# A hybrid decoder block on one core: how the attention values are multiplied, where the probabilities are scaled, and where both stand in TensorE's order

## What is computed

```python
scores = jnp.einsum('bnqgrd,bnkgd->bgrnqk', qb, kk)          # 128 queries x 256 keys a block
scores = jnp.where(valid, scores, -jnp.inf)
m = jnp.maximum(jnp.max(scores, axis=-1, keepdims=True), sink)
pexp = jnp.exp(scores - m)
probs = pexp / (jnp.sum(pexp, axis=-1, keepdims=True) + jnp.exp(sink - m))
out = jnp.einsum('bgrnqk,bnkgd->bnqgrd', probs, vv)
```

## Time and profile before

| | us |
|---|---|
| median of 3 executions | 2165.63 |
| lowest, highest | 2164.36, 2166.37 |
| the profiled execution, its own time | 2168.98 |
| span of the profiled execution | 2167.4 |
| granted TensorE clock, mean over the span | 0.984 |

### The profile page before, as it was taken

How to read it: one execution, slowest core, us unless ns; L and a number is a source line. 1 busy time by engine, 2 the same in 40 slices (tenths; PEclk the granted TensorE clock), 3 DMA queues, 4 the chain that set the end, 5 groups by cost and what they waited for, 6 DMA issues and landing times. The chain is left out here.

```text
span 2167.4 us, 29054 instructions
## 1 busy us (share of the span) xinstructions
PE 2090.6 (96%) x10218; PEld 1739.7 (80%) x10218; DVE 1307.5 (60%) x1824; ACT 844.0 (39%) x1589; POOL 598.4 (28%) x600
## 2 busy tenths in 40 slices
PE   7999999979999999999979999999999999999997
PEld 6888889967878778778758888887888888878885
DVE  6854552237767767777743344558887777752523
ACT  5332221024454444454443222434444443443432
POOL 1000011146576666565610000004222222100000
PEclk9999999989999999999989999999999999999998
DMA  6122241223443433443355434321222222355343
GB/s 225 62 90 97 87 166 69 84 85 129 119 125 117 124 114 124 124 131 97 95 175 179 141 134 145 122 94 72 88 87 71 75 87 87 138 161 195 112 151 88
DMA packets 131264, 252.73 MB, mean 117 GB/s; under 512 B 25264, under 2 KB 70448, under 8 KB 131152
## 3 DMA queue, kind: packets, MB, share of 16 engines
q1 hardware_dynamic: 85584, 174.98, 24.9%
q0 software_dynamic: 15360, 55.32, 7.5%
q10 hardware_dynamic: 30208, 20.98, 3.0%
HBM read 189.63 MB, written 61.60 MB: 116 GB/s over the span
## 5 line engine op out<-in xcount | busy, mean ns | idle before, releaser
L155 PE MATMUL ps_zg<-u_hi,g_hi 128*128 128x512 f32 x448 | 186.0, 415 | 0.0
L157 PE MATMUL ps_zg<-u_hi,g_lo 128*128 128x512 f32 x448 | 177.1, 395 | 0.0
L156 PE MATMUL ps_zg<-u_lo,g_hi 128*128 128x512 f32 x448 | 176.2, 393 | 0.0
L2057 DVE TENSOR_TENSOR lt_d_lo<-lt_w_raw,lt_d_hi 128x640 fp32r<-128x640 f32 (+1 forms) x64 | 57.1, 892 | 147.2 <-ACT lt_d_hi L1782 142.5
L973 POOL TENSOR_TENSOR mx_seg<-mx_seg,mx_cbm 128x1024 f32<-128x1024 f32 x32 | 76.0, 2376 | 161.3 <-DVE mx_cbm L1130 161.3
L155 PE MATMUL ps_zg<-z_w,u_hi 128*128 128x512 f32 x256 | 108.6, 424 | 7.1 <-DVE mx_silu L1155 6.9
L155 PE MATMUL lt_ps<-lt_h_hi,lt_w_hi 128*128 128x512 f32 x256 | 100.7, 393 | 14.8 <-DVE lt_h_lo L2095 13.6
L157 PE MATMUL ps_zg<-z_w,u_lo 128*128 128x512 f32 x256 | 102.3, 400 | 0.0
L156 PE MATMUL ps_zg<-z_w,u_hi 128*128 128x512 f32 x256 | 101.8, 398 | 0.0
L1782 ACT ACTIVATE lt_d_hi<-lt_w_raw 128x640 fp32r<-128x640 f32 (+1 forms) x64 | 50.6, 791 | 130.5 <-PE lt_ps L157 119.6
L1656 POOL TENSOR_TENSOR lt_t_f<-lt_w_raw 128x512 f32<-128x512 f32 x21 | 29.1, 1385 | 261.7 <-DVE lt_t_lo L1985 260.2
(11 more groups left out here) (390 smaller groups left out, 6229.8 us busy)
## 6 DMA issues: line engine op xcount, KB each, us to landing
lt_w_raw<-in_w_up SPq DMA_DIRECT2D x44, 512.0 KB, 4.5
mx_a_row<-acs_s SPq DMA_DIRECT2D x32, 512.0 KB, 3.9
g_raw<-in_w_xbc SPq DMA_DIRECT2D x24, 512.0 KB, 3.2
lt_sig<-gate_s SPq DMA_DIRECT2D x24, 512.0 KB, 3.6
lt_w_raw<-in_w_down SPq DMA_DIRECT2D x32, 384.0 KB, 3.2
ff_s<-lt_fo SPq DMA_DIRECT2D x21, 512.0 KB, 5.0
tok_s<-fr_work POOLq DMA_DIRECT2D x20, 512.0 KB, 3.8
lt_w_raw<-in_w_down SPq DMA_DIRECT2D x32, 320.0 KB, 2.9
```

The source lines that it names most:

```text
L155: pe.matmul(dst, s_hi, m_hi, start=first, stop=False)
L156: pe.matmul(dst, s_hi, m_lo, start=False, stop=False)
L157: return pe.matmul(dst, s_lo, m_hi, start=False, stop=last)
L2057: dve.tensor_tensor(d_lo[:, m % 2, 0:n], w_raw[:, m % 2, 0:n], d_hi[:, m % 2, 0:n].bitcast(F32), ALU.subtract).then_inc(dw_lo_done, 1)
```

## The change

- `values` takes the value block as the weights (64 columns) and the turned probabilities of two heads as the moving operand (256 columns). The output goes to `ps_f` with the head's channels on the partitions: two heads in partitions 0 to 63, two in 64 to 127. It needs no transpose: the transposes of `o_tok`, `o_tok` itself and `attention_out` are gone, and `outputs` copies `o_t` from `ps_f` behind `pv_done`.
- The probabilities are scaled by 1/denominator before they are turned, by four copies with a scale on ScalarE, behind the gate's copy and store (and at c = 7 behind the high parts of the z weights). VectorE makes the reciprocal behind the state update, ahead of the sum of y.
- The transposes of the probabilities stand behind all 24 z products (k = 0 to 7) instead of behind 9 of them.
- `values` of n-1 stands behind gate products 0 to 3 instead of ahead of them, and waits for `ps_f`: for the state update of n-1, or at the end of a group for the copy of the outputs of n-2. The transposes of q and k no longer wait for `o_ready`.

The diff, cut to its core:

```diff
@@ scalar: outputs @@
-                act.wait_ge(o_turned, n + 1)
+                act.wait_ge(pv_done, n + 1)
@@ scalar: group @@
                     act.activation(sink_e[:], mx[:, 1], ACT.Exp).then_inc(sink_done, 1)
...
                     if c == NT - 1 and not last:
                         for k in range(4, KT):
                             split_z(g + 1, k)
+                    act.wait_ge(rden_ready, n + 1)
+                    for r in range(REP):
+                        ins = act.activation(sc[:, r, 0:keys], sc[:, r, 0:keys], ACT.Copy, scale=rden[:, r:r + 1])
+                    ins.then_inc(p_scaled, 1)
                     act.wait_ge(p_turned, n + 1)
@@ vector @@
-            def attention_out(n, opening):
...
-                    if not opening:
-                        attention_out(n - 1, first and c == 1)
...
                         dve.tensor_tensor(state[:], kept[:], ps_f[:], ALU.add).then_inc(state_ready, 1)
+                    dve.wait_ge(sink_done, n + 1)
+                    if not opening:
+                        dve.wait_ge(p_scaled, n)
+                    do(dve.tensor_tensor(rden[:], sums[:], sink_e[:], ALU.add))
+                    dve.reciprocal(rden[:], rden[:]).then_inc(rden_ready, 1)
                     dve.wait_ge(diag_done, n + 1)
...
-                    dve.wait_ge(sink_done, n + 1)
-                    do(dve.tensor_tensor(rden[:], sums[:], sink_e[:], ALU.add))
-                    do(dve.reciprocal(rden[:], rden[:]))
@@ tensor: values @@
-                pe.wait_ge(p_ready, NT * g + c + 1)
+                n = NT * g + c
+                pe.wait_ge(p_ready, n + 1)
+                if c < NT - 1:
+                    pe.wait_ge(state_ready, (NT - 1) * g + c + 1)
+                else:
+                    pe.wait_ge(o_out, n)
                 j, blocks = c % 2, 1 if c == 0 else 2
-                for r in range(REP):
-                    for b in range(blocks):
-                        block_of = c if b == j else c - 1
-                        last = pe.matmul(ps_a[:, r * HD:(r + 1) * HD], p_t[:, r, b], v_in[:, block_of % 4],
+                for b in range(blocks):
+                    block_of = c if b == j else c - 1
+                    for h in range(2):
+                        last = pe.matmul(ps_f[h * HD:(h + 1) * HD, 0:2 * P].rearrange("p (a n) -> p a n", a=2),
+                                         v_in[:, block_of % 4], p_t[:, 2 * h:2 * h + 2, b],
                                          start=(b == 0), stop=(b == blocks - 1))
                 last.then_inc(pv_done, 1)
@@ tensor: turn_outputs @@
-                pe.wait_ge(o_ready, n + 1)
...
-                for a in range(2):
-                    last = pe.transpose(ps_f[:, a * P:(a + 1) * P], o_tok[:, a * P:(a + 1) * P], ident[:])
-                last.then_inc(o_turned, 1)
@@ tensor: group @@
                     if not opening:
+                        gate(g, c, range(0, 4), opening)
                         values(*before)
-                    if not opening:
-                        gate(g, c, range(0, 4), opening)
...
-                    if not opening:
-                        pe.wait_ge(o_ready, n)
...
-                    next_z(g, c, last_group, range(0, 3))
-                    pe.wait_ge(exp_done, n + 1)
+                    next_z(g, c, last_group, range(KT))
+                    pe.wait_ge(p_scaled, n + 1)
                     for r in range(REP):
                         for b in range(keys // P):
                             last = pe.transpose(ps_s[:, r // 2, r % 2, b * P:(b + 1) * P], sc[:, r, b * P:(b + 1) * P], ident[:])
                     last.then_inc(p_turned, 1)
-                    next_z(g, c, last_group, range(3, KT))
```

More of the change, by code:

```diff
@@ L853, in mixers @@
             s.sem(n) for n in "gated sq_done v_ready r0_ready yn_ready y_turned y_out".split())
-        rotated, qk_turned, q_ready, scored, masked, max_ready, exp_done, sink_done, p_turned, p_ready, pv_done, o_ready, o_turned, o_out = (
-            s.sem(n) for n in "rotated qk_turned q_ready scored masked max_ready exp_done sink_done p_turned p_ready pv_done o_ready o_turned o_out".split())
+        rotated, qk_turned, q_ready, scored, masked, max_ready, sink_done, rden_ready, p_scaled, p_turned, p_ready, pv_done, o_out = (
+            s.sem(n) for n in "rotated qk_turned q_ready scored masked max_ready sink_done rden_ready p_scaled p_turned p_ready pv_done o_out".split())
         dve_own, pool_own, act_own = s.sem("dve_own"), s.sem("pool_own"), s.sem("act_own")
@@ L1051, in group @@
                     for r in range(REP):
[L1052 to L1054 removed]
+                        act.activation(sc[:, r, 0:keys], sc[:, r, 0:keys], ACT.Exp, bias=negm[:, r:r + 1],
+                                       accum_out=sums[:, r:r + 1])
                     act.activation(sink_e[:], mx[:, 1], ACT.Exp).then_inc(sink_done, 1)
```

18 lines of the change are left out of this document (1 added, 17 removed).

## The result

The changed kernel is slower: 2172.55 us median (2170.12 to 2181.47, 9 runs) against 2166.37 us of the kernel before (2164.36 to 2168.45, 9 runs), a ratio of 1.0034 with a 95% interval of 1.0022 to 1.0045. That is 6.2 us where 6.5 less were forecast. The profiled execution of after took 2172.38 us, span 2170.8, 3.4 us more than the span of before.

The account below looks back on a forecast made before the run. PE was taken as the bound, its matmuls busy 96% of the span. 24 full steps from 19.8 to 19.3 us gain 12, boundaries cost 3, the end 2.5: net -6.5, so 2159 us, range 2150 to 2174.

Parts of the forecast that it names:

- Parts 1 and 2: PE's work per step: old value products and output transposes go, 1.84 us; four new value products take 1.07 us.
- V: Time of the new value products on PE in a step: taken as 1.07 us, bounds 0.85 and 1.9.
- the serial case: Rival: the four value products run one after the other, V = 1.9, 19.8 us a step, 2166 us; chance 0.2.
- Part 3: Turn behind all z products: turn to k copied takes 7.2 us, PE waits 0.5 for k, full step 19.3.
- The odd steps' gate split becomes the bound: Rival: PE waits 1.2 us for VectorE's product with silu in 12 odd steps, 2174 us; chance 0.22.
- Part 4: Scaling on ScalarE: four copies take 1.1 to 1.6 us, just covered in odd steps; reciprocal delays y about 0.4.
- Part 5: Values behind four groups of gate products: loads and GpSimd's rotation come 2 us later, costing nothing; may even help.
- Part 6: Boundaries and end: three boundaries cost 3 us together, the last step about 2.5 us.
- The clock, the prediction's last rival: Longer boundary idle may lengthen PE's low clock, up to 3 us at each of three boundaries; no chance of its own.

Follow-up runs that it names:

- e7: The changed kernel with the four edits of e1, e2, e3 and e5 together: 2146.66 us, ratio to before 0.9909.
- e8: The changed kernel with e4's order and all four value products written to the lower half of the output partitions (output misplaced): 2183.06 us, one execution.
- e1: The changed kernel with the gate weights' split moved from the head of the odd step to the end of the even step before: 2166.98 us.
- e14: The kernel of e7 with the gate split taken back to the head of odd steps: 2171.59 us, ratio to before 1.0029.
- e2: The changed kernel with the turn of the probabilities behind 18 of the 24 z products instead of all: 2166.39 us.
- e5: The changed kernel with SP's loads freed by the values of n-1 instead of n: 2172.49 us, ratio to before 1.0028.
- e3: The changed kernel with the reciprocal behind the sum of y and its product with silu at the boundaries: 2169.18 us.
- e15: The kernel of e7 with the boundary's reciprocal taken back ahead of the sum of y: 2148.00 us, ratio to before 0.9913.
- e10: The kernel before with only the turn of the probabilities moved behind all 24 z products: 2220.66 us, ratio to before 1.0249.
- e9: The kernel of e7 with the last step's scales ahead of the gate's copy and store on ScalarE: 2145.07 us, ratio to before 0.9905.
- e4: The changed kernel with both key blocks' value products for one half of the output partitions issued before the other half's: 2171.28 us, one execution.
- e6: The changed kernel with the edits of e2 and e5 together: 2175.35 us, ratio to before 1.0037.

## Why the prediction was wrong

**Parts 1 and 2 were right.** V is 1.01 us (705.09 to 706.10 above) where 1.07 was taken and 0.85 to 1.9 were the bounds; the pairs start 7 ns apart. Without waits a step takes 18.88 us (e7); the prediction had "With V = 1.07 PE alone would need 19.0 us a step." e8 shows the serial case at 0.64 us a step more. By the rule of the Trainium skill in "TensorE: Matmul & The Clock Gate", Part 3, V would have been near 1.7, by the estimate of the prediction; the measured 1.01 speaks against that reading of it for column halves, and agrees with the twofold column tiling that "TensorEngine Tiling (Array Packing)" names for 64 weight columns in its section on when to use tiling.

**Part 3's main chain was right**, even steps better than it: turn to k copied 7.0 us (701.38 to 708.37, where k's copy ends) for 7.2, PE's own work 6.9 for 6.7, so that a wait of 0.15 is left of the 0.5. The step is 18.99 for 19.3.

**The step that failed is how the odd steps were priced.** The prediction knew the second chain, from k to the end of VectorE's product with silu, priced it at 1.2 us a step in a rival, and then set it aside on an estimate of 6.6 us against PE's 6.5. It takes 7.33. VectorE's timeline of the changed kernel answers to the earlier trace rows, and ScalarE's k to the earlier trace rows:

```profile
727.08 0.27 ACT L1033 ACTIVATE mx_k_t<-mx_ps_a 128x128 f32<-128x128 f32 x1
...
737.33 1.71 ACT L1065 ACTIVATE mx_sc<-mx_sc,mx_rden 128x256 f32<-128x256 f32 x4 [0.56 <-DVE mx_rden L1162]
```

```profile
728.94 1.50 DVE L1098 TENSOR_TENSOR g_lo<-g_raw,g_hi 128x1024 fp32r<-128x1024 f32 x1 [2.59 <-ACT g_hi L1017]
730.36 1.28 DVE L1130 SCALAR_TENSOR_TENSOR mx_sc<-mx_ps_s,band 128x512 f32<-128x512 f32 x2
...
732.93 0.54 DVE L1140 TENSOR_TENSOR mx_mx<-mx_mx,mx_sinks 128x4 f32<-128x4 f32 x1
733.50 0.52 DVE L1141 TENSOR_SCALAR mx_negm<-mx_mx 128x4 f32<-128x4 f32 x1
...
734.00 0.68 DVE L1145 TENSOR_TENSOR mx_silu<-ps_zg,mx_silu 128x512 f32<-128x512 f32 x1
```

```profile
732.86 0.59 POOL L933 TENSOR_TENSOR mx_m<-mx_qk,cos_t 128x192 f32<-128x192 f32 x1 [3.50 <-DMA mx_bc_f<-feat_s]
```

Term by term, behind k's end at 727.35: the split starts 1.59 later (foretold 1.59), 1.42 pass to the mask (1.4), and from mask to product it is 3.64. I took 2.92 from the last step, the only one in which GpSimd has no rotation to do. In the full step it had been 3.50 already by the prediction's own reading (3.58 from the mask's row, which starts at 730.31), with GpSimd beside it, and that was the row to take: 7.2 us, a wait of 0.7 in every odd step, 8 us over the twelve. That alone turns the forecast of 6.5 less into some 2 more. e1 takes the split out of this chain and the wait before z goes; e14 has all but e1 and keeps the loss.

In the terms of the sum, 4.4 us were forecast to be gained in the even steps and 7.6 in the odd ones, c = 1 among them. Measured were 8.2 gained and 3.3 lost: the odd steps miss by 11 us, the boundaries by 3 and the end by 1, and the even and c = 0 steps give 5 of that back.

**The rival named this bound, and its time is luck in part.** "The odd steps' gate split becomes the bound" had 2174, and 2172.55 was measured. But it put a wait of 1.2 us in each odd step, where 0.3 to 0.9 was found and in one step none, and took the 24 steps for 3 us lost where they gained 4.9; boundaries and end cost 9.3 for its 5.5.

**Part 3 also priced k's chain by one step alone.** With the turn last this chain has no slack, so what GpSimd adds to VectorE's norm steps reaches PE: 0.8 to 1.35 us before the scores in three of the four c = 1 steps of the changed kernel (ahead of the longest, two operations of the norm take 0.65 and 1.39 us instead of 0.16 and 0.75), and up to 1.9 in e1. "PE now waits 0.5 us for k" was read from one pair of steps of a chain whose terms vary. e7 works because e2 gives this chain slack and e1 shortens the other. e1 alone moves the wait to k, e2 alone leaves waits before z, and 5.6 and 6.2 became 26 with the other two.

**Part 4 was right for the full steps**: four scales take 1.71 us, a little over the 1.1 to 1.6, and in odd steps end at 739.04, 1.3 us ahead of the turn. No even step waits for them.

**Part 5 was right by itself**: the loads come 2 us later (GpSimd's wait 3.50 for 1.54), and e5, which more than undoes that, changes nothing. That it "may even help" was wrong: the rotation at 732.86 starts on top of the small steps, 0.54 and 0.52 us. Before, they were nearly as slow in this step, and quick in the last one, where GpSimd has no rotation to do. VectorE's timeline of before, from both:

```profile
732.87 0.47 DVE L1150 TENSOR_TENSOR mx_mx<-mx_mx,mx_sinks 128x4 f32<-128x4 f32 x1
733.38 0.52 DVE L1151 TENSOR_SCALAR mx_negm<-mx_mx 128x4 f32<-128x4 f32 x1
...
1093.31 0.16 DVE L1150 TENSOR_TENSOR mx_mx<-mx_mx,mx_sinks 128x4 f32<-128x4 f32 x1
1093.50 0.17 DVE L1151 TENSOR_SCALAR mx_negm<-mx_mx 128x4 f32<-128x4 f32 x1
```

**Part 6 was too low.** Boundaries cost 5.9 us for 3. PE's timeline at the first boundary answers to the earlier trace rows, those of VectorE and GpSimd stand behind it:

```profile
610.47 1.10 PE L1285 MATMUL mx_ps_e<-mx_state,mx_bc_f 128*128 128x512 f32 x2 [1.09 <-ACT mx_y_t L998]
614.86 0.50 PE L155 MATMUL ps_zg<-z_w,u_hi 128*128 128x512 f32 x1 [1.56 <-DVE mx_silu L1145]
...
619.84 0.50 PE L155 MATMUL ps_zg<-z_w,u_hi 128*128 128x512 f32 x1 [0.37 <-DVE z_w L1094]
622.74 0.51 PE L155 MATMUL ps_zg<-z_w,u_hi 128*128 128x512 f32 x1 [1.24 <-DVE z_w L1094]
```

```profile
616.44 0.16 DVE L1161 TENSOR_TENSOR mx_rden<-mx_sums,mx_sink_e 128x4 f32<-128x4 f32 x1 [1.04 <-ACT mx_sink_e L1053]
...
619.06 5.08 DVE L1094 TENSOR_TENSOR z_w<-raw_pieces,z_w 128x512 fp32r<-128x512 f32 x4
```

```profile
619.91 2.23 POOL L954 TENSOR_TENSOR mx_seg<-mx_a_row,mx_acs_g 128x1024 f32<-128x1024 f32 x1
```

Two waits are new. The C state waits 1.09 us for `y_t`, which leaves its bank behind two splits on ScalarE. They stood there before as well, and then `y_t` was ready 0.14 us ahead of PE; the lost lead makes it late. And the low parts of z's weights come late. The reciprocal, moved ahead of them, waits 1.04 us for the sinks' exponential; and then two of the four take 2.38 and 1.53 us instead of 0.72 beside GpSimd's product, which in the kernel before began behind the last of them (5.08 us for four, 3.00 before). "The reciprocal moved ahead delays y by about 0.4 us" in Part 4 had looked at full steps alone. e3, which starts the low parts earlier and has only one of them slowed, takes 3.4 us off; e15 does not show it again.

The clock, the prediction's last rival, went the other way. In the three boundary steps the granted clock was 0.86, 0.82 and 0.93 before and is 0.93, 0.88 and 1.00 after, though PE idles more there. By clock and length that is some 20 us at 1.2 GHz before and 11 after; at the price of e10, where 3.6 us of it make a step 1.5 us longer, the boundaries would have cost up to 4 us more at an equal clock (an estimate, and at most, since a low clock costs nothing in an idle). The same code can get either clock. The first boundary of e7, then of e9, which are alike there, in the windows view (the clock is the third number from the end):

```profile
600.82:623.52 22.70, 20.25 (x101) 14.76 (x100) 14.32 (x25) 15.06 (x36) 18.76 (x19) 0.92 0.44 133
```

```profile
601.61:622.77 21.16, 18.92 (x101) 13.76 (x100) 15.04 (x24) 14.01 (x35) 18.79 (x19) 1.00 0.46 138
```

So a difference of 1.5 us in one boundary of two profiled executions shows nothing about an edit.

The end cost 3.35 us for 2.5:

```profile
1099.09 1.09 PE L1300 MATMUL mx_ps_s<-ident,mx_sc 128*128 128x128 f32 x8 [3.36 <-ACT mx_sc L1065]
1101.30 1.97 PE L1238 MATMUL mx_ps_f<-mx_p_t,mx_v_in 128*64 128x256 f32 x8 [1.11 <-ACT mx_p_t L1071]
1104.04 1.11 PE L1249 MATMUL mx_ps_e<-ident,raw_pieces 128*128 128x128 f32 x4 [0.77 <-DVE raw_pieces L1183]
```

Of these waits only the first has grown (0.42 us before); the other two also stand in the kernel before. The four scales take 1.71 us there, where 1.3 was taken.

**What stays open.** The medians lie 6.2 us apart, the profiled executions 3.4, and the steps explain the 3.4. The rest goes with the clock: the profiled execution of before had a mean granted clock of 0.984 and was 2.6 us above its median, and of 58 further executions of it eight at 0.984 took 2169.0 us in the mean and 15 at 0.987 took 2165.1; the profiled execution of after had 0.986, the highest of its nine. What decides the clock of an execution was not found. The second boundary takes longer than the others in most of the runs, by a wait that the profile puts down to issue, at the loop's jump (1.7 to 5.5 us in all profiled executions but that of e10); nothing here was tried on it.

## What to carry to other kernels

When PE's work shrinks, price every chain that was covered by the old work, each with the durations that it has beside its neighbours on the other engines in that very step, not with the ones of a quiet step. A kernel that has become bound by two chains gains little from shortening one, so edits that give 0 to 6 us alone may be worth 26 together: take them back one at a time from the best version as well as adding them one at a time to the worst. And a step that is moved behind its cover needs the same look at what consumes it next (e10 lost 54 us, most of it to the wait for one copy and to a clock that was lower in eight of its full steps).

## What the hardware showed that was not expected

- Products that write different halves of the output partitions run side by side though they use the same input rows, whatever their order: 1.02 us for four of 256 columns (e4), 1.01 (changed kernel), 1.73 if all write the same half (e8).
- Small operations of VectorE beside GpSimd last until an operation of GpSimd is over: 0.88 us for 128 elements instead of 0.16 (e1), 1.12 and 1.19 us for two operations on 128x4 at a boundary. In the 17 traces 1034 operations of this stage on 128x4 or 128x1 took over 0.1 us more than the shortest of their kind, and every one of them ended 0.01 to 0.03 us behind the end of an operation of GpSimd. Larger ones are slowed too, 1.82 us for 128x512 instead of 0.68 (e6). No run took GpSimd's work away from beside them, so what a move of it would give is not shown.
- With a PE idle of 1.11 us in every full step the clock dropped in eight of the 24 (e10): the step with a granted clock of 0.92, part of it at 1.2 GHz, takes 22.59 us beside one of 21.04 at 1.00 throughout, 1.5 us more. In the changed kernel, with waits of mostly 0.15 us before the scores and of 0.3 to 0.9 before z in all odd steps but one, the 90 us window above is at 1.00; in e14, with 0.30 and 0.84 in each odd step, so are 530 to 600 us, but a c = 1 step with 0.27 and 2.07 is at 0.93. Which of the two differences between e10 and these, the size of the idle or its place, brings the drop was not tried.
